# Attention stage of a decoder kernel: earlier requests for weight slices, another order on VectorE, row tiles begun one slot sooner

## The reference

```python
def _odd_layer(x, pos, mk, mv, attend, norm_g, w_in, qn, kn, w_out, mem_qn):
    ...
    q = _rope(_rms(heads(q, AT_HEADS), qn), pos)
    k = _rope(_rms(heads(k, AT_KV_HEADS), kn), pos)
    ...
    yC = attend(q, k, v, qi, wi, ki).reshape(B, T, AT_W) * jax.nn.silu(g_c)
    ...
    y = jnp.concatenate([yC, yX.astype(yC.dtype)], axis=-1) @ w_out
    return x + y.astype(x.dtype), (k, v, ki)

def _sparse_attend(q, kg, vg, valid):
    ...
    s = jnp.einsum('bqngd,bqknd->bqngk', qg, kg).astype(jnp.float32) * Dh ** -0.5
    s = jnp.where(valid[:, :, None, None, :], s, -jnp.inf)
    p = jax.nn.softmax(s, axis=-1).astype(vg.dtype)
    return jnp.einsum('bqngk,bqknd->bqngd', p, vg).reshape(B, Q, H, Dh)
```

## Time and profile before

| | |
|---|---|
| median of 3 runs | 1878.97 us (1877.37 to 1880.25) |
| profiled execution, its own time | 1880.33 us |
| its span, first to last instruction | 1878.7 us |
| mean granted TensorE clock | 0.979 of full speed |
| PE / PEld / DVE / ACT / POOL busy | 95% / 73% / 52% / 32% / 22% |
| `layer1_back` | about 1459 us to 1879 us |

### The profile page before, as it was taken

How to read it: one execution, slowest core, us unless ns; L and a number is a source line. 1 busy time by engine, 2 the same in 40 slices (tenths; PEclk the granted TensorE clock), 3 DMA queues, 4 the chain that set the end, 5 groups by cost and what they waited for, 6 DMA issues and landing times. The chain is left out here.

```text
span 1878.7 us, 26519 instructions
## 1 busy us (share of the span) xinstructions
PE 1782.1 (95%) x9417; PEld 1378.5 (73%) x9417; DVE 978.8 (52%) x2277; ACT 601.4 (32%) x1275; POOL 412.4 (22%) x643
## 2 busy tenths in 40 slices
PE   6999999999999998999999999999999689899999
PEld 5666888777788876887876566887767466677887
DVE  5412643233377665221632567888879755685111
ACT  3111342111022112210321346777735445543010
POOL 4301221000133353000342001211005445330000
PEclk9999999999899999999999999999999889999999
DMA  6333333444355467321322122334443764332331
GB/s 214 125 118 121 116 115 108 147 158 128 120 164 181 154 187 280 135 90 42 116 67 79 41 74 69 114 98 138 130 148 113 265 196 135 101 101 85 109 117 46
DMA packets 134637, 236.97 MB, mean 126 GB/s; under 512 B 28486, under 2 KB 61158, under 8 KB 134506
## 3 DMA queue, kind: packets, MB, share of 16 engines
q1 hardware_dynamic: 110938, 172.35, 28.4%
q0 software_dynamic: 17184, 55.85, 9.3%
q10 hardware_dynamic: 6384, 7.08, 1.1%
HBM read 169.05 MB, written 66.17 MB: 125 GB/s over the span
## 5 line engine op out<-in xcount | busy, mean ns | idle before, releaser
L1212 PE MATMUL layer_acc<-layer_w_hi,layer_xT_hi 128*128 128x512 f32 x640 | 262.7, 410 | 0.2 <-PE all_banks L1360 0.2
L1214 PE MATMUL layer_acc<-layer_w_hi,layer_xT_lo 128*128 128x512 f32 x640 | 253.8, 397 | 0.0
L1213 PE MATMUL layer_acc<-layer_w_lo,layer_xT_hi 128*128 128x512 f32 x640 | 253.2, 396 | 0.0
L2784 PE MATMUL front_acc<-front_w_hi,front_xT_hi 128*128 128x512 f32 x520 | 218.1, 419 | 10.4 <-DVE front_w_lo L3325 4.9
L2785 PE MATMUL front_acc<-front_w_lo,front_xT_hi 128*128 128x512 f32 x520 | 206.5, 397 | 0.0
L2786 PE MATMUL front_acc<-front_w_hi,front_xT_lo 128*128 128x512 f32 x520 | 206.2, 397 | 0.0
L1212 PEld LDWEIGHTS layer_acc<-layer_w_hi,layer_xT_hi 128*128 128x128 f32 x640 | 122.2, 191 | 30.7 <-issue 5.9
L1213 PEld LDWEIGHTS layer_acc<-layer_w_lo,layer_xT_hi 128*128 128x128 f32 x640 | 121.7, 190 | 26.7 <-issue 2.6
L1214 PEld LDWEIGHTS layer_acc<-layer_w_hi,layer_xT_lo 128*128 128x128 f32 x640 | 121.2, 189 | 27.1
L2784 PEld LDWEIGHTS front_acc<-front_w_hi,front_xT_hi 128*128 128x128 f32 x520 | 98.6, 190 | 43.1 <-issue 11.8
L3110 ACT ACTIVATE front_index_rows<-odd_bias,front_candidate 128x1024 bf16<-128x1024 f32 (+3 forms) x128 | 124.9, 981 | 8.7 <-DVEq L3474 5.0
(11 more groups left out here) (675 smaller groups left out, 3594.9 us busy)
## 6 DMA issues: line engine op xcount, KB each, us to landing
all_w<-in_w_even POOLq DMA_DIRECT2D x80, 256.0 KB, 3.9
h_even<-layer_st SPq DMA_DIRECT2D x79, 256.0 KB, 2.1
all_w<-in_w_odd POOLq DMA_DIRECT2D x61, 256.0 KB, 3.6
h_odd<-front_st SPq DMA_DIRECT2D x55, 256.0 KB, 2.0
layer_scratch<-h_even SPq DMA_DIRECT2D x46, 256.0 KB, 3.1
all_scratch<-in_w_mem SPq DMA_DIRECT2D x32, 256.0 KB, 3.9
all_scratch<-h_even SPq DMA_DIRECT2D x32, 256.0 KB, 3.6
all_scratch<-x SPq DMA_DIRECT2D x14, 512.0 KB, 3.7
```

The costliest lines, as they stand in the source:

```text
L1212: T.matmul(out[0:rows, :], xh[:, kk, to], wh[:, r, :], start=(kk == 0), stop=False)
L1213: T.matmul(out[0:rows, :], xh[:, kk, to], wl[:, r, :], start=False, stop=False)
L1214: ins = T.matmul(out[0:rows, :], xl[:, kk, to], wh[:, r, :], start=False, stop=(kk == KC - 1))
L2784: T.matmul(out[0:rows, :], xh[:, k, to], wh[:, r, :], start=(k == 0), stop=False, skip_group_check=True)
```

## The change

It has three parts, all in `layer1_back` and its plan.

- POOL asks for the first four weight slices in slot 32 of its own stream, in the `smp` generator (`w == 8` there), and no longer in slot 39 at the first turn of `weights`. The wait ahead of them is the same.
- DVE: prep comes last in slots 0 to 5 alone; from slot 6 on it stands ahead of the job.
- `START[p]` is one less for p = 4 to 8, and `TURN[p]` one more. The squares on ACT, the sums on DVE and POOL's chain move up by one slot, while PE turns the tile in the same slots as before.

```diff
 LATE_TIES = (5, 4)
 
 
-def back_plan(early=(), job_first=False):
+def back_plan(prep_first=(), prep_last=()):
 
     plan = [[] for _ in range(77)]
-    for s in early:
+    for s in prep_first:
         plan[s].append("prep")
     for s in range(1, 40):
         plan[s].append("smp")
-    if job_first:
-        for g in range(67):
-            plan[g].append("job")
     for s in range(57):
-        if s not in early:
+        if s not in prep_first and s not in prep_last:
             plan[s].append("prep")
-    if not job_first:
-        for g in range(67):
-            plan[g].append("job")
+    for g in range(67):
+        plan[g].append("job")
+    for s in prep_last:
+        plan[s].append("prep")
     for s in (3, 5, 7, 9, 10, 11, 13, 15, 17, 18):
         plan[s].append("ties")
     for s in range(39, 65):
@@ -3717,8 +3715,8 @@
     width = lambda g: (block_of(g) + 1) * P
     halves = lambda g: [(k, min(512, width(g) - k)) for k in range(0, width(g), 512)]
     first_half = [sum(len(halves(j)) for j in range(g)) for g in range(JOBS + 1)]
-    START = {p: max(1, 8 * p - 18) for p in range(2, T1)}
-    TURN = {p: 5 if p == 2 else 6 for p in START}
+    START = {p: max(1, 8 * p - (18 if p < 4 else 19)) for p in range(2, T1)}
+    TURN = {p: 5 if p == 2 else 6 if p == 3 else 7 for p in START}
     STEPS = [[(p, s - START[p]) for p in range(2, T1) if 0 <= s - START[p] < TURN[p] + 3] for s in range(57)]
     unit = lambda u: (u // 8, u // 4 % 2, u % 4)
     seq_of = lambda u: 4 * (u // 8) + u % 4
@@ -4045,12 +4043,13 @@
                     if w == 4:
                         pool.wait_ge(pvd, 1)
                         load_v(6, range(PAGES))
+                    if w == 8:
+                        pool.wait_ge(ktr, 2 * (UNITS - 2))
+                        for n in range(RAW):
+                            load_slice(n)
                     yield
 
             def weights():
-                pool.wait_ge(ktr, 2 * (UNITS - 2))
-                for w in range(RAW):
-                    load_slice(w)
                 yield
                 yield
                 for w in range(2 * OUT_CHUNKS):
@@ -4063,7 +4062,7 @@
                     pool.wait_ge(wsd, w - RAW + 1)
                 k, half = divmod(w, 2)
                 pool.dma_start(raw[w % RAW], a["w_out_odd"][:, k, 512 * half:512 * half + 512]).then_inc(w_in[w % RAW], 16)
-            follow(back_plan(early=range(6)), 0, None, prep=preps(), smp=smps(), job=idle(), ties=idle(), weights=weights(), out=idle())
+            follow(back_plan(prep_first=range(6)), 0, None, prep=preps(), smp=smps(), job=idle(), ties=idle(), weights=weights(), out=idle())
 
         @block.tensor
         def _(pe):
@@ -4558,7 +4557,7 @@
                         lower(j + 1)
                     sums(j)
                     yield
-            follow(back_plan(job_first=True), 0, None, prep=preps(), smp=smps(), job=jobs(), ties=late_ties(), weights=weights(), out=outputs())
+            follow(back_plan(prep_last=range(6)), 0, None, prep=preps(), smp=smps(), job=jobs(), ties=late_ties(), weights=weights(), out=outputs())
 
 
 OUTS = [(1, SEQ, D), (NB, NT, D), (1, 1, NH, HD, HD), (1, 1, NH, HD), (1, 1, NH), (1, NB, NH, HD, HD),
```

## The result

| | before | after | second set: before | second set: after |
|---|---|---|---|---|
| median, us | 1879.06 (6 runs, 1873.86 to 1880.25) | 1868.12 (6 runs, 1865.76 to 1872.71) | 1881.17 (18 runs) | 1871.13 (6 runs, 1868.03 to 1873.65) |
| ratio, 95% interval | | 0.9948 (0.9932 to 0.9965) | | 0.9950 (0.9933 to 0.9967) |
| span of the profiled execution, us | 1878.7 | 1871.1 | | 1866.4 |
| mean granted clock | 0.979 | 0.982 | | 0.985 |

The change gives 10 to 11 us. The prediction was 1870.1, in a range of 1865.0 to 1875.0.

The account below looks back on a forecast made before the run. PE, busy 95% of the span, was taken as the bound, its stop before mix(40) the main loss. Terms 6.96 + 1.63 + 0.3 = 8.9 us off the 1878.97 median gave 1870.1 us, range 1865.0 to 1875.0.

Parts of the forecast that it names:

- Slot 41: PE's stop before mix(40): all 4.54 us goes, plus 2.42 us of slow clock after it, together 6.96 us.
- Its cause: Slot 41: earlier requests end the slice's DMA wait; earlier preparation 7 sums leave POOL idle at the first CAST.
- a POOL still at its gains: First CAST in slot 41 still slow: PE would stop 1.4 us; sum 7.5, or 5.1 if the clock falls.
- The requests inside preparation 6: Requests behind preparation 6's gains delay its rotation by 2.25 us; its chain starts earlier, so nothing waits.
- Preparation 5: PE's wait of 1.63 us for POOL's rotation before its first turn goes, with 3.5 us to spare.
- Preparation 4: PE's 1.45 us wait for POOL goes but moves to the next group, which already waits 1.94 us: gain 0.
- Preparation 3: PE's 1.40 us wait for POOL: START unmoved, sums pass one job; 0.3 us gained, bounds 0 and 1.40.
- Other rows and collisions: Other moved sums and collisions of POOL's gains with DVE: taken as 0, bounds -0.7 to +2.1 us.
- new PE stops of about a microsecond at the moved sums: Sign the prediction is wrong: such stops in slots 14, 22, 30, 38 and 46, or the slots behind them.
- half given back: Rival: sums ahead of the job delay y_of; three of tiles 4 to 8 lose 1.3 us each; 1874.0; chance 0.17.

Follow-up runs that it names:

- e9: Changed kernel with the exponentials' bias of two-half jobs made by tensor_scalar instead of scalar_tensor_tensor; 1868.33 us, ratio 0.9939 to the kernel before.
- e10: The changed kernel itself, run and traced again with no further edit; 1871.13 us, ratio 0.9950 to the kernel before.
- e1: Kernel before with only the four slice requests moved, from slot 40 to slot 32 of the program; 1880.54 us, ratio 1.0003.
- e4: Changed kernel with the slice requests set back to slot 40, order and slots kept as changed; 1871.05 us, ratio 0.9957 to the kernel before.
- e6: Changed kernel with DVE doing the samples' normalisation of slot 19 behind the job, not ahead; 1866.54 us, ratio 0.9938 to the kernel before.
- e7: e6 plus ACT's samples' exponentials in slot 19 moved behind the copies of job 17; 1865.40 us, ratio 0.9930 to the kernel before.
- e5: Changed kernel with DVE's job ahead of prep again in slots 6 and 7, so preparation 3's sums follow job 7; 1872.17 us, ratio 0.9959.
- e8: e1 with the exponentials' bias of two-half jobs made by tensor_scalar instead of scalar_tensor_tensor; 1879.01 us, ratio 0.9986 to the kernel before.
- e11: e7 with the tensor_scalar form of the bias from e8 added; 1865.31 us, ratio 0.9920 to the kernel before.
- e2: Kernel before with only DVE's order changed, prep ahead of the job from slot 6 on; 1872.13 us, ratio 0.9957.

## Why the prediction was right, step by step

**Slot 41: 6.96 predicted, 6.42 net and 7.32 by itself.** The stop of 4.54 us and the slow clock after it are gone. What the sum didn't have is the new collision at 1608.94, which costs 0.9 us (e9 against e10: -7.32 and -6.41).

**Its cause was half right.** The prediction gave the end of the DMA wait to the earlier requests, and the idle POOL to the earlier sums. The runs show that the second does both, and that the first of the three edits has no gain of its own; a number for all three together could not tell this. Requests alone give 3.0 us in slot 41 and pay 1.3 for it in slot 34 (e1); order and slots without them give 6.41 (e4), as the whole change does. In the kernel before the slices were late because POOL was, and POOL because DVE's sums were. The stop that the prediction named for a POOL still at its gains, 1.4 us, was too small: e1 shows 2.14 with the lower clock behind it, because the bias is held too and the split queues behind it.

**The requests inside preparation 6: nothing, right here and only here.** POOL issues them behind the gains at 1583.51, with its chain a slot and a half earlier. In e1, where the chain is where it was, they cost PE 2.02 us.

**Preparation 5: 1.63 predicted, 1.70 measured**, in every kernel that moves its sums, by the order or by the slots.

**Preparation 4: 0 predicted, and the wait did move on.** 1.45 and 1.94 us before, 3.4 together; no wait and then 4.04 after (4.76 in e10). e6 and e7 show that it stood behind the samples' exponentials, as the earlier trace rows had it.

**Preparation 3: 0.3 predicted, with bounds of 0 and 1.40.** Its wait is 1.39 after and 1.40 before: 0. What its earlier sums do give lies elsewhere, in the operation of line 4515 and the clock behind it (e5): 0.2 to 1.9 us over jobs 6 to 12. The prediction had no such term.

**Other rows and collisions: 0 predicted, within -0.7 to +2.1.** The collision of the earlier trace rows is gone in slots 28 to 38 (-0.71), a new one costs 0.9, and jobs 43 to 63 give -0.33. The prediction named new PE stops of about a microsecond at the moved sums as a sign against it, and there are two. In slot 14 the sums of preparation 4 make `y_of` late, as its rival "half given back" had it: a stop of 1.28 us at 1519.88, and jobs 12 to 17 take 18.89 us, 0.4 to 0.9 more than in before, e1 and e8. And behind the sums of preparation 8 PE stops for 1.78 us at 1641.97, because the low part of a split takes 3.34 us beside POOL's gains and not 0.69:

```profile
1638.07 3.34 DVE L113 TENSOR_TENSOR back_w_lo<-all_w,back_w_hi 128x512 fp32r<-128x512 f32 x1
```

There it cost nothing on balance: before, PE stopped for 0.81, 0.74 and 1.21 us in the same jobs. Behind the sums moved to slots 22, 30 and 38 no new stop stands, apart from the 0.81 us of the collision above. So the zero for the moved rows held roughly as a net, and not place by place; that the pieces cancelled is luck.

From job 27 to 63 this makes 9.16 us, where the terms there were 6.96 + 1.63 = 8.6. The medians' 10 to 11 us are 1 to 2 more. Of the part up to job 27 the runs show a gain at preparation 3 (0.2 to 1.9) and a loss at preparation 4 (0.4 to 0.9); together jobs 6 to 17 take 40.6 to 40.8 us in the seven traces with both edits and 40.1 to 41.7 in before, e1 and e8. Whether that or the scatter makes up the rest, no run here tells.

## What to carry over

When a transfer is late, ask who was late in asking: a request that stands behind computed work on the issuing engine is cured by making that work earlier, and moving the request alone may only shift its own cost of issue (2.2 us for four) onto something else. When a wait is removed and the next group takes it over, as in slot 20, the next edit is already named: put the late waiter behind the job on both engines. Before a difference of 2 us between two profiles is explained, look at a trace of a kernel that has no edit there; and where a whole stretch scatters, look at short ones inside it, which here repeated well enough to show a stop of 1.28 us that the sums of preparation 4 had brought.

## What the runs showed of the hardware that I hadn't expected

- One small operation of DVE, 128 x 1 with two tensors from SBUF, took 0.22 us alone and 0.67 to 2.37 beside GpSimd's tensor_tensor of 128 x 1024, and it ended within 0.04 us of that instruction: begun 1.15 us into it, it took 1.23 (after); 1.72 us into it, 0.67 (before, at 1653.97); 0.01 us ahead of it, 2.37 (e1). Beside GpSimd's power of 128 x 10, which takes 1.96 us, it took its normal 0.22. As a tensor_scalar with both operands as per-partition scalars it took 0.27 at every place beside one (e8, e9, e11).
- The length of a stop alone doesn't say whether the clock falls. After 2.14 us in e1 the next group took 2.37 in place of 1.59; after 2.52 us in e6 it took its normal 0.94; after 1.59 us in e2 its normal 1.58. At one and the same place, the wait for preparation 6's rotation, 2.02 us in e1 left the clock at 1.00 and 2.03 us in e8 was followed by a group of 1.74 us in place of 1.28.
